# Cutting 640 token columns into matmuls of 512 and 128 instead of 320 and 320, in a two-layer diffusion trunk

## What is computed

```
m = silu(cond) @ mod_w + mod_b                     -> shift, scale, gate for three steps
x = x + 0.5 * g1 * swiglu(norm(x)*(1+sc1)+sh1)     w1, w3: 1024 x 2816; w2: 2816 x 1024
h = norm(x)*(1+scm)+shm
x = x + gm * (W_out [attention | gated conv | DeltaNet | 2-D DFT](h @ W_in))   W_in: 1024 x 2576
x = x + 0.5 * g2 * swiglu(norm(x)*(1+sc2)+sh2)
swiglu(h) = (silu(h @ w1) * (h @ w3)) @ w2
```

## Time and profile before

| what | value |
|---|---|
| median of two runs | 3556.2 us (3553.93 and 3558.47) |
| span of the profiled execution | 3559.9 us |
| TensorE matmul busy | 3252.2 us, 91% |
| VectorE, ScalarE, GpSimd busy | 1512.8, 876.7 and 294.5 us |
| mean granted TensorE clock | 0.914 of full speed |
| data moved | 258.77 MB, 73 GB/s |

### The profile page before, as it was taken

How to read it: one execution, slowest core, us unless ns; L and a number is a source line. 1 busy time by engine, 2 the same in 40 slices (tenths; PEclk the granted TensorE clock), 3 DMA queues, 4 the chain that set the end, 5 groups by cost and what they waited for, 6 DMA issues and landing times.

```text
span 3559.9 us, 54453 instructions
## 1 busy us (share of the span) xinstructions
PE 3252.2 (91%) x21815; PEld 3035.6 (85%) x21815; DVE 1512.8 (42%) x2402; ACT 876.7 (25%) x1254; POOL 294.5 (8%) x253
## 2 busy tenths in 40 slices
PE   4999998987799989999979999989878999899997
PEld 2899998974588789999959999989547888799997
DVE  1444445233445444444333444351444554444444
ACT  2312222232322322121122222132233323222121
POOL 1000001000224210000010000010003331000001
PEclk6999999996688899999979999999877879899998
DMA  6333331220000032222253333212100001222221
GB/s 223 112 118 118 118 118 59 72 68 3 2 2 0 12 108 71 71 71 71 95 178 118 118 118 118 94 48 63 56 1 4 0 0 60 95 71 71 71 71 42
DMA packets 218173, 258.77 MB, mean 73 GB/s; under 512 B 11804, under 2 KB 204420, under 8 KB 217696
## 3 DMA queue, kind: packets, MB, share of 16 engines
q1 hardware_dynamic: 215648, 250.56, 21.4%
q0 software_dynamic: 2432, 6.96, 0.6%
HBM read 254.34 MB, written 3.15 MB: 72 GB/s over the span
## 4 chain that ended last, share of the span: by engine, by line
issue 65%; PE 26%; DVE 3%; POOLq 2%; POOL 1%; DMA 1%; DVEq 1%; ACT 0%; SPq 0%; ACTq 0%
PE ps L495 15%; PE ps L508 8%; POOLq L406 2%; POOL dB L473 1%; PE ps L846 1%; PE ps L742 1%; DMA ub<-mixer_tables 0%; DVE ast L1445 0%; DVE pexp L1454 0%; DMA PT<-x_sample 0%; DVEq L1223 0%; PE ps L786 0%; DVE cv L1412 0%; DVE PT L1491 0%; PE ps L612 0%
## 5 line engine op out<-in xcount | busy, mean ns | idle before, releaser
L508 PE MATMUL ps<-hh,uh 128*128 128x320 f32 x3744 | 866.1, 313 | 41.7 <-DVE hl L1252 32.0
L508 PE MATMUL ps<-hl,uh 128*128 128x320 f32 x3744 | 860.7, 311 | 0.0
L508 PE MATMUL ps<-hh,ul 128*128 128x320 f32 x3744 | 859.2, 311 | 0.0
L508 PEld LDWEIGHTS ps<-hh,uh 128*128 128x128 f32 x3744 | 632.0, 190 | 56.1 <-DVE hl L1252 33.4
L508 PEld LDWEIGHTS ps<-hl,uh 128*128 128x128 f32 x3744 | 633.7, 190 | 0.0
L508 PEld LDWEIGHTS ps<-hh,ul 128*128 128x128 f32 x3744 | 632.6, 190 | 0.0
L1262 DVE SCALAR_TENSOR_TENSOR xT<-ps,modT,xT 128x128 f32<-128x128 f32 x736 | 371.4, 547 | 313.7 <-PE ps L508 312.8
L1214 DVE TENSOR_TENSOR ul<-raw,uh 128x1024 fp32r<-128x1024 f32 x322 | 390.1, 1234 | 265.5 <-ACT uh L945 245.1
L945 ACT CAST uh<-raw 128x1024 fp32r<-128x1024 f32 x322 | 323.8, 1046 | 447.9 <-PE ps L508 412.9
L1282 DVE TENSOR_TENSOR PT<-ps,PT 128x640 f32<-128x640 f32 x88 | 72.5, 824 | 739.0 <-PE ps L508 739.0
L508 PE MATMUL ps<-gh,uh 128*128 (+1 forms) x1408 | 326.5, 313 | 14.2 <-DVE ul L1214 14.2
(11 more groups left out here) (221 smaller groups left out, 2746.4 us busy)
## 6 DMA issues: line engine op xcount, KB each, us to landing
raw<-ffn_w SPq DMA_DIRECT2D x264, 512.0 KB
PT<-mod_w SPq DMA_DIRECT2D x72, 1024.0 KB, 6.3
raw<-w_in SPq DMA_DIRECT2D x40, 512.0 KB
raw<-w_out SPq DMA_DIRECT2D x8, 768.0 KB
ub<-mixer_tables POOLq DMA_DIRECT2D x2, 2176.0 KB, 8.5
out<-PT SPq DMA_DIRECT2D x5, 512.0 KB, 2.7
PT<-x_sample SPq DMA_DIRECT2D x1, 2048.0 KB, 13.3
raw<-w_out SPq DMA_DIRECT2D x16, 128.0 KB
```

Source lines behind the costliest of these rows:

```text
L508: last = pe.matmul(pair(q)[:, lo:hi], wt[:, wk * P:(wk + 1) * P], mv(mk, lo, hi), start=start and i == 0 and p_ == 0, stop=stop and i == n ...
```

## The change

The two stretches are now columns 0 to 511 and 512 to 639, and `pair(q)` begins at the start of bank 2q, so that the first stretch fills that bank and the second takes the first 128 columns of the next. Nothing else is touched: the number of matmuls and of weight loads, the order, the semaphores and the readers' instructions stay. Roots and reciprocals, which follow HALVES, are also cut at 512.

```
-HALVES = ((0, 320), (320, 640))
+HALVES = ((0, 512), (512, 640))
...
         def pair(q):
-            return ps_all[:, q * 1024 + 192:q * 1024 + 832]
+            return ps_all[:, q * 1024:q * 1024 + 640]
```

## The result

The changed kernel takes 3907.5 us (median of two runs, 3906.3 and 3908.7) against 3556.2 us: 1.0985 times as long, 95% interval 1.0939 to 1.1032. Its profiled execution has a span of 3904.8 us against 3559.9, 344.9 us more. The forecast was 3935.

The account below looks back on a forecast made before the run. TensorE was taken as the bound, through the start-to-start time of L508's matmuls. The terms 371 + 10 - 2 - 1 + 1 = +379 us on the median of 3556 gave 3935 us, with a range of 3870 to 4840.

Parts of the forecast that it names:

- The bound: Whole kernel: TensorE's L508 sets the time, so nearly every nanosecond added to a pair of its matmuls comes out at the end.
- The 128-column matmul at the price of a load (112 ns): L508's short matmul: its stream cannot cover the next weight load, so it costs 112 ns; this case had chance 0.70.
- The 512-column matmul at 230 ns: L508's long matmul: taken as 230 ns, between 226.7 and 234.7, with ample cover for the load.
- The starts should alternate, about 230 after a 512-column matmul and about 112 after a 128-column one.: Sign in L508's timeline; the forecast is wrong if the interval after the short matmul is under 90 or over 150 ns.
- How many, and at which clock: L508: 7633 pairs at full clock at 48.6 ns more each, 371 us; 95 pairs at the lower clock, 10 us.
- 95 x 107 ns: L508 after some ten pauses: 95 pairs at the lower clock, each 107 ns longer, 10 us.
- What hides it: L508's 56 us of waits mostly stay; -2.4 us at four feed-forward ends, -1 us in the first projections.
- Roots, plain fp32, readers: Seven norms' roots add 1.4 us; plain fp32 matmuls on HALVES change within 1 us of nothing; evacuations not at all.
- the DeltaNet and attention stretches should keep their lengths: Sign in the profile outside L508's steady stretches: the DeltaNet and attention parts take as long as before.
- No fast mode: Rival, L508's short matmul: runs no faster than plain fp32, 213 to 223 ns; 4750 us, up to 4840; chance 0.22.
- hidden load: Rival, L508: the next long matmul's weights are fetched during the 512-column stream; time stays 3556 us; chance 0.06.
- cheaper streams: Rival, L508: only each short load costs the extra 13.4 ns, the pair is 272 ns; 3390 us; chance 0.02.

Follow-up runs that it names:

- the runs with shorter loads: Changed kernel with 64 weight columns instead of 128 in most matmuls of one length: 3628.7 us for the 512-column ones, 3911.2 us for the 128-column ones.
- the third matmul: Changed kernel with L508 cut in three, 512 + 64 + 64 columns, so a third matmul and third load in each group: 6719.6 us.
- the grouped run: Changed kernel with a chunk's three products looped inside the stretches, so three long matmuls, then three short ones: 3924.9 us.

## Why the prediction was right, and where it was not

**The bound.** Right. TensorE's L508 sets the time before and after, and the loss of a pair came out at the end almost undiminished: 46.4 ns a pair in the second feed-forward.

**The 128-column matmul at the price of a load (112 ns).** Right in the sum, and shown by the runs with shorter loads, the third matmul and the 448 + 192 cut. The row that carried it, fp32r weights loaded behind a 2-column matmul in 0.11 us, holds for a stream of fp32r as well: its loads come every 0.11 us.

**The 512-column matmul at 230 ns.** Right: 0.23 us in the grouped run. The pair was forecast at 342 ns and is 340.

**"The starts should alternate, about 230 after a 512-column matmul and about 112 after a 128-column one."** Wrong: 280 and 60. By its own test (under 90 after the short one) the forecast would have counted as wrong, although its pair was right: the two intervals were off by about 50 ns each, in opposite directions. The failing step was to read a matmul's recorded start as the start of its stream. In the earlier trace rows this can't be seen, since a run of matmuls that all wait for loads has equal intervals whichever end is booked. The test should have named the starts of the loads.

**How many, and at which clock.** Here lies most of the 28 us by which the forecast was too high. Summed over the starts of L508 in the two traces, without its long waits, the part at full clock rose from 2238 to 2606 us: +368, forecast +371. The part at the lower clock fell from 63.5 to 50.2 us: -13, forecast +10. A pair at that clock was sized right, 640 ns, as the changed kernel's timeline has it from 689.10 to 689.74:

```profile
689.10 0.84 PE L508 MATMUL ps<-hl,uh 128*128 128x512 f32 x2
689.74 0.84 PE L508 MATMUL ps<-hh,ul 128*128 128x512 f32 x2
```

But only about 77 pairs ran at it, against 116 before. The term that failed is "95 x 107 ns": it held the number of such pairs fixed. In the traces what holds is the time: L508's stretches at the lower clock last 4.2 us on average before and 4.1 after (63.5 us in 15 of them, 50 in 12), so longer pairs mean fewer in each. The rest is that there were three stretches fewer, and no run shows why.

**What hides it.** Nearly right. L508's waits for the others are 32.3 + 14.2 + 8.5 = 55 us where they were 56. At a feed-forward's end the forecast said that GpSimd would vanish as releaser and 0.6 us go. It did not vanish: the sums come every 2.04 us with TensorE's outputs, but each is still the last to be ready (changed kernel's timeline, answering to the earlier trace rows; the row's own wait fell from 2.52 to 1.52 us, so 1.0 us went and not 0.6):

```profile
674.18 1.56 POOL L405 TENSOR_TENSOR PT<-PT 128x640 f32<-128x640 f32 x1 [0.46 <-ACT PT L951]
...
676.22 1.53 POOL L405 TENSOR_TENSOR PT<-PT 128x640 f32<-128x640 f32 x1 [0.48 <-ACT PT L951]
...
677.81 2.43 PE L495 MATMUL ps<-PT,tb 128*128 128x512 f32 x8 [1.52 <-POOL PT L405]
...
680.27 0.95 ACT L956 ACTIVATE PT<-ps,tb 128x512 f32<-128x512 f32 x2 [0.79 <-PE ps L495]
680.99 3.35 DVE L1222 RECIPROCAL PT<-PT 128x512 f32<-128x512 f32 x1 [3.66 <-ACT PT L956]
```

**Roots, plain fp32, readers.** Right: the eight plain fp32 matmuls of the sums take 2.43 us for 2.42, the first root now leads the reciprocal by 680.99 - 680.27 = 0.72 us instead of 0.56, and the reciprocal of 512 columns takes 3.35 us. That "the DeltaNet and attention stretches should keep their lengths" holds only for the sum of the mixer's two stretches. The two mixer stretches before and after:

```profile
767.00:1231.00 464.00, 391.92 (x2384) 318.93 (x2383) 227.50 (x442) 137.78 (x248) 106.24 (x89) 0.77 0.02 8
2517.70:2972.00 454.30, 379.77 (x2385) 311.45 (x2383) 227.42 (x442) 137.75 (x248) 106.21 (x89) 0.80 0.02 8
```

```profile
862.30:1314.30 452.00, 377.82 (x2384) 306.93 (x2382) 227.37 (x442) 137.56 (x248) 106.37 (x89) 0.80 0.02 8
2773.70:3238.30 464.60, 391.51 (x2384) 317.82 (x2382) 227.29 (x442) 137.77 (x248) 106.34 (x89) 0.77 0.02 8
```

Each is about 453 us at a mean clock of 0.80 or about 464 at 0.77, in either kernel and in either layer; the sums are 918 and 917. Differences of 10 us between single stretches are this and not the change.

**The rivals.** "No fast mode" (0.22, 4750 us) is out: the pair takes 340 ns and not 446 or more, and four cycles a column would make 192 columns longer than 128, while 448 + 192 is cheaper. The hidden load (0.06) and the cheaper streams (0.02) are out by the load starts and by the time itself. Two of the forecast's numbers don't follow from their own terms, without weight in the outcome: 213 ns for the short matmul would make that first rival's pair 443 and not 446, and a pair of 337 gives about 3897 us and not 3890. The range's upper part, from 4095 on, stood for the first of them alone and rested on the lack of any fp32r row under 320 columns; the rule of the Trainium skill that was weighed ("TensorE: Matmul & The Clock Gate", "LDWEIGHTS (loading the stationary operand)", weight columns over 1.2) was borne out at full clock, with loads 0.11 us apart. At the lower clock the runs have 256 cycles of 0.83 ns, 213 ns, where the rule gives 107 whatever the clock. The other rule of the Trainium skill that was weighed (same page, "Back-to-back issue gap", columns over 2.4 plus 2.5 ns) is given there for the gap of an isolated matmul, with other figures for a stream of weight loads and matmuls. Its 272 ns a pair was not met here: the kernel before takes 293 and the changed one 340.

## What to carry to other kernels

Where every matmul brings its own weight load, a matmul costs the larger of its stream and the next load, so a fixed number of columns should be cut so that no part falls under a load's length (here 256 columns for 128 fp32r weight columns). For 640 columns the even cut does that, and filling a PSUM bank brought nothing that made up for the short rest. Read the price of a load where almost nothing streams, and look for exposed loads in the starts of the loads and not of the matmuls, as a matmul's record takes in the wait for its weights. And count the stretch at the lower clock after a pause in time, since here it was not a fixed number of instructions.

## What the runs showed that was not expected

The cut in three lost the full clock for whole stages: 1355 us at 0.50 with L508 on record for 1350.86 of them, and the same in the second layer, while the same groups of L508 ran at 1.00 in the feed-forward before. The recorded busy time says nothing of it. The trace does show what TensorE did when the clock changed. First two stretches of the first feed-forward that ran at the lower clock (stretch, length, PE, PEld, DVE, ACT, POOL, then the granted clock), then TensorE's rows where the clock rose and where it fell; in between, from 224 to 888 us, it was 1.00:

```profile
100.00:220.00 120.00, 120.00 (x424) 106.32 (x423) 20.56 (x31) 15.49 (x22) 0.00 (x0) 0.50 0.10 34
...
890.00:930.00 40.00, 40.00 (x142) 35.44 (x142) 9.24 (x16) 5.16 (x7) 9.25 (x6) 0.50 0.17 53
```

```profile
220.32 3.23 PE L531 MATMUL ps<-PT,condP 128*32 128x256 f32 x32
...
885.42 0.62 PE L508 MATMUL ps<-gh,ul 128*128 x3
889.59 0.79 PE L508 MATMUL ps<-gh,uh 128*128 128x512 f32 x1 [3.55 <-DVE ul L1214]
```

Groups of L508 alone ran at the lower clock up to a row of 32 matmuls of the modulation (L531). During these the full clock was granted, and it stayed, also through stretches of up to 44 us of L508 alone. A wait of 3.55 us ended it, and it did not come back while only L508 ran. The second layer shows the same (L531 from 3552.53 us, a wait from 4217.85), and the second feed-forward of either layer has no L531 inside. In the changed kernel no stretch of L508 at the lower clock was longer than 6.8 us. No run tested what the clock follows, so the cause stays open.

Open too is what the nanoseconds beyond the cycles at full clock are. They are 147 - 133 = 13 for 320 columns before, 0.23 us - 213 = about 17 for a covered 512, and 340 - 320 = 20 for a pair of 512 + 128; at the lower clock there are none (0.64 us is 768 cycles of 0.83 ns). Over the 7728 pairs of the kernel before, 27 ns each are some 200 us, and no cut that was tried won time from them.
